# First tile's output projection and routing ahead of the other two in a one-core encoder step

## The reference

```
xn  = rmsnorm(x, norm1_g);  z = xn @ w_in           # B | C | h | q | k | v | 2 gates
a   = (B * dwconv3(C * h)) @ w_conv_out
b   = attention_out @ w_attn_out                    # 8 heads, two softmaxes subtracted, block-causal
x1  = x + (sigmoid(gA) * a + sigmoid(gB) * b) @ w_o
xs  = rmsnorm(x1, norm2_g)
q   = rmsnorm((xs @ peer_wq) as 8 heads x 256)      # two halves of 128 a head
s   = q . subkeys (128 keys a half);  top 16 of each half;  top 16 of the 16 x 16 sums
w   = softmax(best 16);  experts = 128 * key0 + key1
y   = x1 + sum over 128 of  w * gelu(u[expert] . xs) * v[expert]
```

## Time and profile before

| | us |
|---|---|
| median of three runs | 3870.24 |
| the profiled execution | 3871.54 |
| its span, first to last instruction | 3869.7 |
| PE busy | 3173.4 (82%) |
| DVE busy | 2519.2 (65%) |
| POOL busy | 1503.4 (39%) |
| ACT busy | 1457.9 (38%) |
| moved by DMA | 1340.70 MB, 1108.54 of them by the gathers' queue |

### The profile page before, as it was taken

How to read it: one execution, slowest core, us unless ns; L and a number is a source line. 1 busy time by engine, 2 the same in 40 slices (tenths; PEclk the granted TensorE clock), 3 DMA queues, 4 the chain that set the end, 5 groups by cost and what they waited for, 6 DMA issues and landing times.

```text
span 3869.7 us, 46441 instructions
## 1 busy us (share of the span) xinstructions
PE 3173.4 (82%) x14521; PEld 1452.5 (38%) x14521; DVE 2519.2 (65%) x5855; ACT 1457.9 (38%) x4432; POOL 1503.4 (39%) x1410
## 2 busy tenths in 40 slices
PE   7999988788988999797888788878879667666666
PEld 4555545344434554353333333545335111111111
DVE  4332016888888964777777786886578754556664
ACT  3222002356753244223556564234323333333333
POOL 2110002356654432424445555433354433344442
PEclk9999999899998999898889998889989776666676
DMA  5223336799999999999899999999999999999998
GB/s 179 93 84 110 102 121 265 294 380 376 418 399 392 413 417 387 407 342 346 318 355 391 357 365 407 418 415 418 404 419 418 385 420 419 420 420 419 411 420 337
DMA packets 252964, 1340.70 MB, mean 346 GB/s; under 512 B 27344, under 2 KB 66032, under 8 KB 117296
## 3 DMA queue, kind: packets, MB, share of 16 engines
q0 software_dynamic: 152400, 1108.54, 70.8%
q1 hardware_dynamic: 94320, 215.23, 15.2%
q10 hardware_dynamic: 6000, 13.96, 1.0%
HBM read 1310.49 MB, written 27.15 MB: 346 GB/s over the span
## 4 chain that ended last, share of the span: by engine, by line
PE 46%; DMA 25%; DVE 14%; ACT 8%; issue 3%; DVEq 2%; POOL 1%; ACTq 1%; SPq 0%; POOLq 0%
DMA mix<-in_peer_uv,tl_idx 14%; PE tl_ps L1012 9%; PE tl_ps L958 9%; DMA ringx<-in_peer_uv,tl_idx 9%; PE tl_ps L791 7%; PE tl_ps L939 4%; PE tl_ps L995 4%; PE tl_ps L971 3%; PE tl_ps L856 3%; PE tl_ps L766 2%; DVE ringx L1650 2%; DVE mix L1650 2%; PE tl_ps L825 2%; DMA mix<-in_peer_uv,tl_itop 1%; DVE xa L1661 1%
## 5 line engine op out<-in xcount | busy, mean ns | idle before, releaser
L712 POOL DMA_INDIRECT ringx<-in_peer_uv,tl_idx x568 | 671.2, 1182 | 912.9 <-PE tl_ps L1012 625.6
L1650 DVE CUSTOM_DVE_ANT_0 ringx<-ringx,xb 128x1024 f32<-128x1024 f32 x585 | 708.2, 1221 | 295.4 <-DMA ringx<-in_peer_uv,tl_idx 263.7
L1012 PE MATMUL tl_ps<-ringx,tl_dg 64*64 64x512 f32 x3808 | 655.4, 774 | 284.7 <-ACT tl_dg L1244 269.0
L712 POOL DMA_INDIRECT mix<-in_peer_uv,tl_idx x456 | 550.1, 1206 | 791.5 <-PE tl_ps L1012 470.5
L1233 ACT ACTIVATE tl_hg<-tl_hd 128x1 f32<-128x1 f32 x1056 | 213.3, 202 | 1428.9 <-DVE tl_hd L1650 1412.1
L1650 DVE CUSTOM_DVE_ANT_0 mix<-mix,xb 128x1024 f32<-128x1024 f32 x471 | 571.4, 1221 | 242.3 <-DMA mix<-in_peer_uv,tl_idx 216.6
L1012 PE MATMUL tl_ps<-mix,tl_dg 64*64 64x512 f32 x2832 | 477.8, 757 | 233.9 <-ACT tl_dg L1244 232.2
L958 PE MATMUL tl_ps<-tl_xr,low 128*128 128x384 f32 (+1 forms) x1280 | 403.4, 472 | 3.1 <-DVE tl_xr L1608 3.1
L1012 PEld LDWEIGHTS tl_ps<-ringx,tl_dg 64*64 64x64 f32 x3808 | 120.8, 156 | 682.0 <-ACT tl_dg L1244 571.7
L1237 ACT ACTIVATE tl_hw<-tl_hg,tl_gw 128x1 f32<-128x1 f32 x1024 | 301.5, 294 | 74.0 <-issue 4.7
L958 PEld LDWEIGHTS tl_ps<-tl_xr,low 128*128 128x128 f32 x1280 | 248.2, 197 | 172.5 <-issue 43.5
(11 more groups left out here) (205 smaller groups left out, 3876.9 us busy)
## 6 DMA issues: line engine op xcount, KB each, us to landing
low<-in_wall SPq DMA_DIRECT2D x240, 512.0 KB, 7.8
low<-in_watt SPq DMA_DIRECT2D x60, 512.0 KB, 8.6
ringx<-in_peer_uv,tl_idx POOLq DMA_INDIRECT x568, 14.7
mix<-in_peer_uv,tl_idx POOLq DMA_INDIRECT x456, 14.7
ringx<-in_watt SPq DMA_DIRECT2D x12, 512.0 KB, 6.8
u<-in_x_prompt SPq DMA_DIRECT2D x8, 512.0 KB, 11.1
x_rows<-u SPq DMA_DIRECT2D x8, 512.0 KB, 7.7
xs_rows<-u SPq DMA_DIRECT2D x8, 512.0 KB, 7.5
```

The costliest lines, as they stand in the source:

```text
L712: nc.gpsimd.indirect_dma_start(out=ring[q % RING].rearrange("p a d -> p (a d)"), out_offset=None, in_=A["peer_uv"], in_offset=bass.Indirec ...
L1012: last = nc.tensor.matmul(ps[half_of(h), b, :], dg[rows, npe(q) % DIAGS, :], ring[q % RING][rows, 1, h * 512:(h + 1) * 512], start=k == 0, ...
L1650: nc.vector.tensor_tensor_reduce(out=ring[q % RING][:, 0, :], in0=ring[q % RING][:, 0, :], in1=xb[:, t % 2, :], scale=1.0, scalar=0.0, op0 ...
```

## The change

Only block 1 (tiles 0 to 2) and the due times are touched. w_o is done in pieces: six blocks for tile 0, four for tiles 1 and 2, the last two for tile 0, the last four for the others. Tile 0's row work follows at once, with x1 in `xa` and xs in `xb`, where the experts' slots read them, so that tile 0 is neither stored nor loaded. Its transposes and the first four query blocks (128 columns) come ahead of the others' transposes; their small products use PSUM banks 0 and 1. VectorE searches these, and unit 0 of the routing (now at -3.1, in steps of 0.2) follows. Then the same four weight blocks are used again for tiles 1 and 2 (256 columns), and the other twelve for all three. Those lie from slot 1.2 to 25.4. The store of xn_t moves to load 30. Block 2's attention and middle begin 4 slots later, block 3's 29 slots later; most of the routing units move along, those of tiles 4 (second) and 5 stay, and SHARED stays.

```
-ATT = ((-330, 1.0), (25.5, 0.75), (337, 0.93))
+ATT = ((-330, 1.0), (29.5, 0.75), (366, 0.93))
...
-PLAN = ((-106.5, 1600, 1600, 7), (172.5, 1, 1750, 7), (520, 1, 1100, 7))
+PLAN = ((-106.5, 1600, 1600, 7), (176.5, 1, 1750, 7), (549, 1, 1100, 7))
...
-UNIT_AT = ((-1.5, 0), (8, 1), (18, 1), (27, 1), (40, 3), (68, 3), (130, 4), (170, 5), (321, 3), (346, 3),
-           (388, 4), (450, 5), (514, 5), (560, 5), (713, 3), (745, 4), (850, 4), (900, 4), (950, 4), (985, 4))
+UNIT_AT = ((-3.1, 0.2), (11.1, 1), (19.9, 1), (28.5, 1), (40, 3), (68, 3), (130, 4), (170, 5), (325, 3), (350, 3),
+           (394, 4), (450, 5), (514, 5), (560, 5), (742, 3), (774, 4), (850, 4), (900, 4), (950, 4), (985, 4))
 NORM_AT, TAB_AT, LAM_AT, KEYS_AT = -326, -325.5, -318, -290
...
+    if rb == 0:
+        ends[40:] = [-1.8 + 0.2 * k for k in range(4)] + [1.2 + 2.2 * k for k in range(12)]
...
+def out_pieces(rb):
+
+    every = tuple(range(3))
+    if rb:
+        return [(c, every) for c in range(DC)]
+    first, others = every[:1], every[1:]
+    return ([(c, first) for c in range(6)] + [(c, others) for c in range(4)]
+            + [(c, first) for c in range(6, DC)] + [(c, others) for c in range(4, DC)])
+
+
+def own_tiles(rb, qb):
+
+    return (1, 2) if rb == 0 and qb < 4 else (0, 1, 2)
...
+                        if rb == 0:
+                            sp.sem_inc(s["x1_out"], 16)
+                            sp.sem_inc(s["xs_out"], 16)
+                        stored = [(i, t) for i, t in enumerate(tiles) if rb or i]
+                        for i, t in stored:
                             sp.wait_ge(s["x_done"], 3 * rb + i + 1)
                             sp.dma_start(rows_in(A["x1"], t), X[:rows_of(t), i, :]).then_inc(s["x1_out"], 16)
...
-                    if m == 50 and rb + 1 < PASSES:
+                    if m == (50 if rb else 30) and rb + 1 < PASSES:
...
+                if rb == 0:
+                    yield -3
+                    pool.wait_ge(s["qss0_done"], 1)
+                    nc.gpsimd.tensor_tensor(rq[:, 0, 0:2], qse[:, 0, 0:2], keep["mhalf"][:, 0:2], ALU.pow).then_inc(s["rq0_done"], 1)
                 for quad in range(4):
-                    yield ends[43 + 4 * quad] + (RQ_LAG if rb or quad else 3)
+                    yield ends[43 + 4 * quad] + (RQ_LAG if rb or quad else 13)
...
-                    for i in range(3):
+                    for i in own_tiles(rb, qb):
...
-                for c in range(DC):
-                    for i, t in enumerate(tiles):
-                        m = rows_of(t)
+                for c, some in out_pieces(rb):
+                    for i in some:
+                        m = rows_of(tiles[i])
...
+                    if 2 in some:
+                        last.then_inc(s["z_done"], 1)
+                    elif c == DC - 1:
+                        last.then_inc(s["w0_done"], 1)
+
+                def turn_rows(i):
...
+                        rows = X[:m, i, :] if rb or i else xb[:, 0, :]
...
+                            last = nc.tensor.transpose(ps[:, 2 + 2 * i + h, c % 4 * P:c % 4 * P + m], rows[:, c * P:(c + 1) * P],
...
+                def small_first(qb):
+
+                    pe.wait_ge(s["q0_cp"], qb + 1)
...
+                    if qb >= 2:
+                        pe.wait_ge(s["tops0_done"], qb - 1)
+                    nc.tensor.matmul(ps[:, qb % 2, P:P + 1], qsq[:, qb % 3, 0:P], ones[:],
+                                     start=True, stop=True, skip_group_check=True)
+                    nc.tensor.matmul(ps[:, qb % 2, 0:P], qT[:, qb % 3, 0:P], skT[:, qb % 2, :],
+                                     start=True, stop=True, skip_group_check=True).then_inc(s["sm0_done"], 1)
+
+                for i in range(3):
+                    yield from turn_rows(i)
+                    if rb or i:
+                        continue
+                    for qb in range(4):
+                        yield turn + 2
+                        if qb == 0:
+                            pe.wait_ge(s["xtc"], 1)
+                        if qb >= 2:
+                            pe.wait_ge(s["q0_cp"], qb - 1)
+                        landed_block(base + 40 + qb)
+                        w = low_block(keep, (base + 40 + qb) % WRING).rearrange("p (c n) -> p c n", c=DC)
+                        for c in range(DC):
+                            last = nc.tensor.matmul(ps[:, 2 + qb % 2, 0:P], w[:, c, :], xT[:, c, 0:P], start=(c == 0), stop=(c == DC - 1),
+                                                    skip_group_check=True)
+                        last.then_inc(s["z0_done"], 1)
+                        if qb:
+                            small_first(qb - 1)
+                    small_first(3)
                 for qb in range(2 * PH):
+                    own = own_tiles(rb, qb)
+                    cols = slice(own[0] * P, n)
...
+                        yield ends[40 + qb] - (DC - c) * (ends[41 + qb] - ends[40 + qb] if qb + 1 < 2 * PH else ends[41 + qb - 1] - ends[40 + qb - 1]) / (DC + 1)
...
+                        last = nc.tensor.matmul(ps[:, 2 + qb % 2, cols], w[:, c, :], xT[:, c, cols], start=(c == 0), stop=(c == DC - 1))
...
-                pe.wait_ge(s["xa_in"], 16 * (t + 1))
+                if t:
+                    pe.wait_ge(s["xa_in"], 16 * t)
+                else:
+                    pe.wait_ge(s["x_done"], 1)
...
+                    rows = X[:m, i, :] if rb or i else xa[:]
...
+                for i in range(3):
+                    yield ends[39] + 3 + i
+                    square_rows(i)
+                    if rb == 0 and i == 0:
+                        keep_rows(0)
+                if rb == 0:
+                    for qb in range(4):
+                        yield turn + 2
+                        act.wait_ge(s["z0_done"], qb + 1)
+                        if qb >= 3:
+                            act.wait_ge(s["sm0_done"], qb - 2)
+                        nc.scalar.activation(qsq[:, qb % 3, 0:P], ps[:, 2 + qb % 2, 0:P], ACT.Square, scale=256 ** -0.5)
+                        nc.scalar.copy(qT[:, qb % 3, 0:P], ps[:, 2 + qb % 2, 0:P])
+                        act.drain().then_inc(s["q0_cp"], 1)
+                for i in range(0 if rb else 1, 3):
+                    yield turn + i + 3
+                    keep_rows(i)
...
+                    yield ends[40 + qb] + 2 if rb or qb > 3 else (-1.5 if qb == 3 else -2)
...
-                    load_row(0)
-                    load_x1(0)
...
+            def find_tops(rb, qb, own=None):
+
+                first = rb == 0 and own == (0,)
+                own = own or own_tiles(rb, qb)
+                if first:
+                    bank = ps[:, qb % 2, :]
+                    src = {0: bank[:, 0:P]}
+                    dve.wait_ge(s["sm0_done"], qb + 1)
+                else:
+                    bank = ps[:, 4 + qb % 3, :]
+                    src = {i: bank[:, i * P:(i + 1) * P] for i in own}
+                    dve.wait_ge(s["sm_done"], 16 * rb + qb + 1)
+                for i in own:
...
-                dve.wait_ge(s["rq_done"], 4 * (t // 3) + (h0 + nh) // 2)
+                if t == 0 and h0 == 0:
+                    dve.wait_ge(s["rq0_done"], 1)
+                else:
+                    dve.wait_ge(s["rq_done"], 4 * (t // 3) + (h0 + nh) // 2)
...
+                    if rb or i:
+                        dve.wait_ge(s["z_done"], base + 40)
+                    else:
+                        dve.wait_ge(s["w0_done"], 1)
+                    out = X[:m, i, :] if rb or i else xa[:]
+                    nc.vector.tensor_tensor(out, ps[:m, 2 + 2 * i:4 + 2 * i, :].rearrange("p a b -> p (a b)"), X[:m, i, :],
...
+                    if rb or i:
+                        dve.wait_ge(s["x1_out"], 48 * rb + 48)
+                    src, out = (X[:m, i, :], X[:m, i, :]) if rb or i else (xa[:], xb[:, 0, :])
+                    nc.vector.scalar_tensor_tensor(out=out, in0=src, scalar=rx[:m, i:i + 1], in1=g2b[:m],
                                                    op0=ALU.mult, op1=ALU.mult).then_inc(s["xn_done"], 1)
+
+                if rb == 0:
+                    yield ends[39] + 2
+                    add_rows(0)
+                    add_eps(0)
+                    norm_rows(0)
+                    for step in (add_rows, add_eps, norm_rows):
+                        for i in (1, 2):
+                            step(i)
+                    for qb in range(4):
+                        find_tops(0, qb, (0,))
+                else:
+                    for i in range(3):
+                        yield ends[39] + 2 + i
...
-                    yield (ends[41 + qb] if qb < 2 * PH - 1 else ends[MID - 1] + 2) + 1
+                    if rb == 0 and qb < 4:
+                        yield qb if qb else -1.5
+                    else:
+                        yield (ends[41 + qb] if qb < 2 * PH - 1 else ends[MID - 1] + 2) + 1
...
+                if k == 0 and t:
+                    dve.wait_ge(s["xb_in"], 16 * t if t < NT else 16 * (NT + 3))
```

(37 more changed lines are left out.)

60 lines of the change are left out of this document (28 added, 32 removed).

## The result

The changed kernel takes 3829.48 us (median of four, 3827.97 to 3836.14), the kernel before 3870.45 (median of four); ratio 0.9899, 95% interval 0.9887 to 0.9912. It is faster by 41 us where 19 were forecast: the direction and the range (3824 to 3874) hold, the gain is more than twice the forecast one. Its profiled execution has a span of 3826.9 us.

What follows compares the result with a forecast made beforehand. Transfers bind from the first gather on, except where engines lag, as VectorE in the first query stage. Gains of 18.9 and 10.1 us less 10 for the third block made 19: 3851 us, own range 3840 to 3862, wider 3824 to 3874.

Steps and rivals of the forecast that it cites:

- Part 1: From w_o to the first gather: tile 0 goes ahead, first gather at 593.5, 33.4 us sooner, 28 to 37 by bounds.
- the split: First block's query stage: splitting 384 columns into 128 and 256 costs TensorE 4.4 us.
- Part 2: First block's query stage: 18.9 us of the earlier gather kept, plus 10.1 us for being four gathers further; 29.0 us persist.
- the four slots: Second block begins at slot 29.5 instead of 25.5: four more products and two thirds of an addition on VectorE, 5.8 us.
- the searches: VectorE's searches of tiles 1 and 2 after the first gather: one free, three more in slots 1 to 3 cost 8.7 us.
- the 11.4: TensorE's second stand before the first gather, 11.4 us until 627.88, waiting for ScalarE; forecast to go.
- four gathers: After the query stage the kernel is four gathers further, at 2.53 us each 10.1 us gained.
- Part 3: Third block 29 slots later: 15 - 19 - 6, a loss of 10 us, between -38 and +20.
- (a): Third block's first attention units: cleared of routing unit 3b, 15 us gained, 0 if the slowness is attention's own start.
- (b): Third block's attention now overlaps unit 5a, costing 19 us, and VectorE's two-thirds share of additions, costing 6 us.
- second rival: The third block's later start costs nothing or gains 15 us: 29 to 44 us in all, 3826 to 3841; chance 0.18.

Runs made afterwards that it cites:

- e7: The changed kernel with the store of xn_t put back at load 50, after query block 4: 3850.47 us, 0.9946 of the kernel before.
- e1: The changed kernel with the third block 4 slots later than before instead of 29: 3852.19 us, 0.9959 of the kernel before.
- e2: The kernel before with only the third block's due times 25 slots later, no new code: 3847.47 us, 0.9951 of the kernel before.
- e9: e1 (third block at +4) with routing unit 3b at slot 366 instead of 350: 3836.24 us, 0.9910 of the kernel before.
- e10: The changed kernel with the third block 8 slots later than before instead of 29: 3838.01 us, 0.9920 of the kernel before.
- e6: The changed kernel with the third block 16 slots later than before instead of 29: 3828.41 us, 0.9898 of the kernel before.
- e8: The changed kernel with units 5a, 5b at 549, 590 and VectorE's two-thirds share in slots 549 to 709: 3819.49 us, 0.9867 of the kernel before.
- e5: The changed kernel with routing unit 3b at 386 instead of 350 and 4a at 414 instead of 394: 3833.04 us, 0.9903 of the kernel before.
- e3: The changed kernel with routing units 5a and 5b at 549 and 590 instead of 514 and 560: 3824.68 us, 0.9882 of the kernel before.
- e11: e8 with the second block another 8 slots later, the third staying at 366: 3821.36 us, 0.9874 of the kernel before.

## Why the prediction was wrong in size

**Part 1, the earlier first gather: right, a little short.** 33.4 us forecast, 39.4 in the profile, 35.4 from w_o's start. The chain was as drawn: add beside w_o, transposes, four narrow blocks, four searches, unit 0. Two rows were read wrongly. I took 0.222 us for a transpose, but those 24 had run after TensorE's stand of 8 us. The window before has the granted clock at 0.54 there (0.50 in its first half, 0.57 in its second), 1.2 GHz but for a part of its end; in the kernel after, the transposes follow w_o without a stand, at 1.00, 2.4 GHz, and eight of them take 1.04 us. Before:

```profile
573.00:579.00 6.00, 5.32 (x24) 4.98 (x24) 2.76 (x3) 2.37 (x5) 0.00 (x0) 0.54 0.81 299
```

After:

```profile
561.00:563.00 2.00, 1.30 (x10) 0.80 (x7) 1.46 (x2) 0.66 (x2) 0.00 (x0) 1.00 0.03 12
```

And 32 instructions of 128 columns take 3.67 us from start to start, 0.115 each, not 0.155; with 0.219 for 256 columns the split costs 64 x (0.115 + 0.219 - 0.326) = 0.5 us, not 4.4. The Trainium skill, "TensorE: Matmul & The Clock Gate", "Back-to-back issue gap", says that the load of the weights and the stream set the spacing together, pipelined. Here the load is nearly hidden at 128 columns too, since 0.115 is close to a third of the 384-column spacing, 0.109.

**Part 2, what is kept: the balance was right, an item was off.** 18.9 us forecast after the query stage; 19.2 in the profile (15.2 without the 4.0). Query stage and four more gathers gave back 20.2 us, not 14.5. I had priced the four slots by VectorE's product and share of additions alone, 5.8 us. At the stage's own pace (121.9 / 34 = 3.6 us a slot) they are 14.3, which would leave 5.9 for the searches, for which I had 8.7; no run parts the two. Of TensorE's standing for ScalarE's copies in this stage, which I took for gone with the 11.4, 11.5 us are left of 14.1. e7 shows that the stage is as long wherever it begins, 142.0 and 142.1 us. The 10.1 us for four gathers were 8.5. Together parts 1 and 2 were 29.0 in the forecast; e1, where they stand alone with both blocks at +4, gives 16 to 18. Its table row says where the rest went: block 2 4.4 us longer than before and the third block's attention 7.9 longer, 5.6 regained in its middle. Unit 4a moved by 6 slots and units 4b to 5b stayed, where the block moved by 4; whether that is the reason was not isolated.

**Part 3, the third block 29 slots later: the step that failed.** Forecast +15 - 19 - 6 = -10; measured +23 (e1 against the changed kernel) or +21 (e2 against before). Term by term. (a), 15 us for clearing attention's start of unit 3b, was right in size for that unit: e9 shows 16. What the sum put at nothing is that attention at 337 also began on the last search of block 2's query stage (due at slot 337) and on unit 3a, which runs to slot 345 (its first slot 321, eight steps of 3; in e1 all of this lies 4 slots later). e10 keeps unit 3b on attention and still gains 14 by four slots; e6 gains it all with 12. So it is not the price of a unit alone but that of a pile: searches, 3a, 3b and attention's start one upon the other. Moving 3b away or moving attention 4 slots off the searches gives about two thirds of it each; 3a was not moved by itself. With (b) out of the way the distance is worth 33 us (e1 against e8), where the sum had 15. (b), 25 us for unit 5a and the share, was mis-sized: 10 (e8). I had derived the price of a unit, 19 us, as the rest of one stretch of 130 us with a unit on it, and carried it to another place whole; e5 and e3 put a unit at 4 to 7 us, neither clear of the noise. What is left open: why 3b costs 16 us under a start at 341 and, put at the same engine on later and heavier units (e5), 4.

The forecast's second rival, "the third block costs nothing, or gains its 15 us: 3826 to 3841", comes nearest to what happened, at 0.18 of the chances. That the time falls inside its numbers is partly luck: its 29 us from parts 1 and 2 were 16 to 18, and its 0 to 15 from part 3 were 21 to 23, two errors that cancel. The same holds for the range of the forecast. The rival's own evidence, 12 gathers in 50 us, was the best row in the prediction, and I let a price estimated from a mean over attention outweigh it.

## What to carry to other kernels

Where all engines follow one fixed order of due times beside a saturated transfer, look first for the places where two stages meet: a few slots of distance there cost nothing in transfers, since they are given back at the end, and were worth as much here (19 to 21 us, four numbers) as the reordering of a whole stage (16 to 18). Not every boundary pays: eight slots at the first one gave nothing (e11). When the work of the engines is tied to slots and its order stays, what is lost at the first transfer of such a stream is lost at the end (e7), whatever the engines could do in the wait. And a price per overlapped piece, taken from one stretch and carried to another, did not hold here: measure the stage where it piles up.

## What the runs showed of the hardware

At full clock (1.00 in the windows of both kernels) a float32 instruction of 128 x 128 with its weight load advances TensorE 0.115 us, one of 256 columns 0.219, one of 384 0.326: time by the column, so that splitting a product by columns was nearly free. The first product comes 6.3 us (before) and 6.5 us (after) behind the issue of its gather.
